# Two networks in one kernel: the gating's offset, the group norm and the masks of the rwkv stage, and who makes the third part of w_lo

## What is computed

```python
def _chunked_sgu(u, v, ln_g, ln_b, w_s, b_s):
    ...
    vn = ((vf - mu) * lax.rsqrt(var + SGU_LN_EPS)).reshape(bsz, t, A_WIDTH)
    vn = (vn * ln_g + ln_b).astype(v.dtype)
    ...
    mixed = jnp.einsum('gts,bcsgd->bctgd', wm, vc) + b_s.T[:, :, None]
    return u * mixed.reshape(bsz, t, A_WIDTH)
...
    y = _rwkv7_scan(rh, wh, kh, vh, kk, ah)
    ym = jnp.mean(y, axis=-1, keepdims=True)
    yv = jnp.mean(jnp.square(y - ym), axis=-1, keepdims=True)
    y = ((y - ym) * lax.rsqrt(yv + RWKV_GN_EPS)).reshape(bsz, t, B_WIDTH)
    y = y * gn_g.astype(jnp.float32) + gn_b.astype(jnp.float32)
    bonus = jnp.sum(rh * kh * r_k.astype(jnp.float32), axis=-1, keepdims=True) * vh
    y = (y + bonus.reshape(bsz, t, B_WIDTH)) * g.astype(jnp.float32)
```

## Time and profile before

| | |
|---|---|
| median of 3 runs | 2133.46 us (2132.8 to 2133.58) |
| the profiled execution | 2138.42 us, its span 2136.6 us |
| granted PE clock, mean | 0.984 of full speed |
| busy: PE, DVE, ACT, POOL | 2036.4, 1579.4, 1150.2, 447.4 us |
| delta's projection, rwkv stage, sparse's projection, from the span's start | about 206 to 296, 1088 to 1300, 1498 to 1594 us |

### The profile page before, as it was taken

One profiled execution on the slowest core, in us unless ns is written; L12 is line 12 of the kernel. 1 busy time (PEld: TensorE's weight loads), 2 busy tenths in 40 slices (PEclk: granted clock), 3 DMA queues, 4 the chain that ended last, 5 costly groups with the idle time before them and its releaser, 6 DMA issues.

```text
span 2136.6 us, 31970 instructions
## 1 busy us (share of the span) xinstructions
PE 2036.4 (95%) x11858; PEld 1778.4 (83%) x11858; DVE 1579.4 (74%) x2157; ACT 1150.2 (54%) x1687; POOL 447.4 (21%) x211
## 2 busy tenths in 40 slices
PE   7999989999999999999999989999987999999997
PEld 6888877888888899888888978888975888888885
DVE  5777886677777778677768476777675488888887
ACT  5445543544454455645455425445445577777775
POOL 2222213232322210133222432323320300000000
PEclk9999999999999999999999999999997999999998
DMA  8555420456555653355543005555450488888895
GB/s 336 186 196 168 152 105 14 169 192 193 190 177 182 198 169 141 138 189 195 187 158 119 1 1 181 193 190 193 158 178 15 166 332 326 326 325 324 326 327 194
DMA packets 73396, 401.23 MB, mean 188 GB/s; under 512 B 8256, under 2 KB 8384, under 8 KB 41152
## 3 DMA queue, kind: packets, MB, share of 16 engines
q1 hardware_dynamic: 72848, 398.07, 53.8%
q10 hardware_dynamic: 432, 1.57, 0.2%
HBM read 398.57 MB, written 1.05 MB: 187 GB/s over the span
## 4 chain that ended last, share of the span: by engine, by line
PE 77%; DVE 12%; PEld 4%; ACT 4%; issue 2%; POOL 1%; DMA 0%; SPq 0%; ACTq 0%; PEldq 0%; DVEq 0%; POOLq 0%
PE psum L737 17%; PE psum L306 13%; PE psum L307 13%; PE psum L308 12%; PE psum L741 9%; DVE w_lo L290 3%; PE psum L958 2%; ACT w_hi L283 2%; PE psum L946 2%; PE psum L320 2%; PE psum L2759 1%; PEld psum L306 1%; PEld psum L308 1%; PEld psum L307 1%; POOL w_lo L296 1%
## 5 line engine op out<-in xcount | busy, mean ns | idle before, releaser
L290 DVE TENSOR_TENSOR w_lo<-ring,w_hi 128x1024 fp32r<-128x1024 f32 x498 | 754.3, 1544 | 185.4 <-ACT w_hi L283 183.9
L283 ACT ACTIVATE w_hi<-ring 128x1024 fp32r<-128x1024 f32 x744 | 739.9, 1051 | 236.5 <-PEq L500 131.3
L296 POOL TENSOR_TENSOR w_lo<-ring,w_hi 128x1024 fp32r<-128x1024 f32 x153 | 381.4, 2493 | 1135.7 <-ACT w_hi L283 1135.7
L737 PE MATMUL psum<-fT,w_hi 128*128 128x512 f32 x1760 | 423.7, 392 | 12.9 <-DVE w_lo L290 10.4
L737 PEld LDWEIGHTS psum<-fT,w_hi 128*128 128x128 f32 x1760 | 330.4, 189 | 84.7 <-issue 7.5
L306 PE MATMUL psum<-w_hi,hT_hi 128*128 128x384 f32 (+4 forms) x896 | 321.7, 359 | 19.8 <-POOL w_lo L296 6.0
L308 PE MATMUL psum<-w_hi,hT_lo 128*128 128x384 f32 (+4 forms) x896 | 310.6, 347 | 0.0
L307 PE MATMUL psum<-w_lo,hT_hi 128*128 128x384 f32 (+4 forms) x896 | 310.3, 346 | 0.0
L306 PE MATMUL psum<-w_hi,act_hi 128*128 128x512 f32 x616 | 242.4, 394 | 5.4 <-DVE act_lo L835 4.6
L307 PE MATMUL psum<-w_lo,act_hi 128*128 128x512 f32 x616 | 241.2, 392 | 0.0
L308 PE MATMUL psum<-w_hi,act_lo 128*128 128x512 f32 x616 | 240.0, 390 | 0.0
(11 more groups left out here) (484 smaller groups left out, 2455.1 us busy)
## 6 DMA issues: line engine op xcount, KB each, us to landing
ring<-in_stream SPq DMA_DIRECT2D x249, 1024.0 KB, 5.6
ring<-in_stream SPq DMA_DIRECT2D x248, 512.0 KB, 4.3
tables<-in_tables SPq DMA_DIRECT2D x1, 2261.0 KB, 19.8
gain_row<-in_gains ACTq DMA_DIRECT2D x3, 512.0 KB, 4.8
rows<-in_rows SPq DMA_DIRECT2D x1, 1288.0 KB, 22.7
X<-in_x SPq DMA_DIRECT2D x1, 1024.0 KB, 5.0
result<-X SPq DMA_DIRECT2D x2, 512.0 KB, 3.4
columns<-in_columns SPq DMA_DIRECT2D x1, 993.0 KB, 14.9
```

The lines of the kernel that those rows point to most:

```text
L283: act.activation(part(w_hi, g, i), ring[:, k, i * PART:(i + 1) * PART], ACT.Copy) \
L290: dve.tensor_tensor(part(w_lo, g, i), ring[:, k, i * PART:(i + 1) * PART], part(w_hi, g, i).bitcast(F32), ALU.subtract) \
L296: pool.tensor_tensor(part(w_lo, g, 2), ring[:, k, 2 * PART:STEP], part(w_hi, g, 2).bitcast(F32), ALU.subtract) \
L737: pe.matmul(psum[:, 4 + 2 * (s % 2) + o, :], w[0][:, o, k, :], fT[:, k, :, :].rearrange("p a c -> p (a c)"), start=k == 0, stop=False, ski ...
```

## The change

Delta and sparse: the third part of w_lo is made by DVE in the projection's steps (`lasts`), and POOL waits until DVE is done. rwkv: the row sums of the gating's weights and the level made of them go; PE adds the product of the weights with ln_b in the same accumulation, POOL multiplies the gate's input by ln_g, and DVE adds sgu_b and multiplies by u in one operation per group out of PSUM. Result y is centred while it is copied from PSUM, with the mean reduced from PSUM. Half 0's variances and the norm of its first tile move into rwkv1's levels (`ahead`, before a level's U). A of half 1 is masked, and its first AM made, in rwkv0's last level. State, right side, solution and results of half 0 and matrices L, R, B move between rwkv1's levels; many `keep_warm` go; the turned tiles are issued one by one; the bonus on ACT moves to rwkv0's levels.

```diff
+        def inverse_begin(dve, A, AM):
             dve.tensor_tensor(AM[:, :, :], A[:, :, :], over(table("level")[:, 0:P], 8), ALU.mult).then_inc(*inverse.vector())
...
             for l in range(1, LEVELS):
+                if l in ahead:
+                    ahead[l]()
...
         def delta_pool(pool, at):
-            proj_pool(pool, first_step[at], len(D_KINDS))
+            pool.wait_ge(lo_last_ready, first_step[at] + len(D_KINDS))
...
-            proj_copies_vector(dve, "delta", at, D_KINDS, d_place, between)
+            proj_copies_vector(dve, "delta", at, D_KINDS, d_place, between, lasts=range(len(D_KINDS)))
...
         def sparse_pool(pool, at):
-            proj_pool(pool, first_step[at], len(N_KINDS) + SPARSE_C)
+            pool.wait_ge(lo_last_ready, first_step[at] + len(N_KINDS) + 1)
+            proj_pool(pool, first_step[at] + len(N_KINDS), SPARSE_C)
...
-                        {3: lambda: rotate(0), 4: lambda: rotate(1), 6: windows}, ahead=True)
+                        {3: lambda: rotate(0), 4: lambda: rotate(1), 6: windows}, ahead=True, lasts=range(len(N_KINDS)))
...
-            b = open_bank(pe, "rwkv sgu rows")
-            for g in range(4):
-                ins = pe.matmul(b[:, g:g + 1], col("sgu_w")[:, g * P:(g + 1) * P], ones[:, 0:1], start=True, stop=True)
-            ins.then_inc(*rwkv.tensor("rwkv sgu rows"))
...
+            def gating(t, gs):
+                b = open_bank(pe, f"rwkv sgu {t}") if gs[0] == 0 else bank(f"rwkv sgu {t}")
+                pe.wait_ge(*after(f"rwkv sgu scaled {t}"))
+                for g in gs:
+                    pe.matmul(b[:, g * P:(g + 1) * P], col("sgu_w")[:, g * P:(g + 1) * P], r_tok[:, t, 512 + g * P:512 + (g + 1) * P], start=True, stop=False)
+                    ins = pe.matmul(b[:, g * P:(g + 1) * P], col("sgu_w")[:, g * P:(g + 1) * P], row("ln_b")[:, g * P:(g + 1) * P], start=False, stop=True)
...
             inverse_tensor(pe, "rwkv0", r_T, r_U[0], r_Y, r_AM, 4, meanwhile=lambda: (matrix(0, "B"), key_rows()),
-                           at_level={5: lambda: right_side(0, 0), 6: lambda: matrix(1, "A")})
...
+                           at_level={5: lambda: (right_side(0, 0), matrix(1, "A"))})
+            solved(0, 0, 2)
+            inverse_tensor(pe, "rwkv1", r_T, r_U[1], r_Y, r_AM, 0, meanwhile=lambda: (state(0), result(0, 0)),
+                           at_level={1: lambda: right_side(0, 1), 2: lambda: (solved(0, 1), matrix(1, "L")), 3: lambda: result(0, 1),
+                                     4: lambda: matrix(1, "R"), 5: lambda: (right_side(1, 0), matrix(1, "B"))})
+            gating(0, range(4))
             solved(1, 0)
+            gating(1, range(2))
             state(1)
             result(1, 0)
-            gating()
             right_side(1, 1)
+            gating(1, range(2, 4))
             solved(1, 1)
+            turn(0, 0)
             result(1, 1)
...
+            turn(1, 0)
+            turn(0, 4)
+
+            out_tensor(pe, "rwkv", at, after_first=lambda: turn(1, 4), turns=1, warm=6)
...
             solved(1, 0)
...
+            split_hi(act, g, g, freed=f"rwkv1 dU {LEVELS - 1} 1")
             right_side(1, 1)
...
+            root(0, 1)
             solved(1, 1)
...
+            out_scalar(act, at, "rwkv", "used rwkv sgu 0", rwkv, meanwhile=lambda: root(1, 1), ahead=True)
...
+            inverse_pool(pool, "rwkv0", r_A, r_AM, at_level={4: lambda: shifted(0), 5: lambda: gate_scaled(0), 6: lambda: gate_scaled(1)})
+            inverse_pool(pool, "rwkv1", r_A, r_AM, at_level={1: lambda: gated(0), 2: lambda: shifted(1), 3: lambda: gated(1), 4: lambda: scaled(0),
+                                                             5: lambda: scaled(1)})
...
             def result(half, c):
                 dve.wait_ge(*after(f"rwkv y {half} {c}"))
-                does(f"used rwkv y {half} {c}", dve.tensor_copy, O[:, c, 512 + 256 * half:768 + 256 * half], bank(f"rwkv y {half} {c}")[:, 0:SEQ])
+                y, mean = bank(f"rwkv y {half} {c}")[:, 0:SEQ], r_stat[:, 5, 8 * c + 4 * half:8 * c + 4 * half + 4]
+                does(None, dve.tensor_reduce, mean, groups(y, 64), AX.X, ALU.add)
...
+            def next_half():
+                dve.wait_ge(*after(f"rwkv0 Y {LEVELS - 1} 1"))
+                masked(1, "A")
+                settle()
+                inverse_begin(dve, r_A, r_AM)
...
+            inverse_vector(dve, "rwkv0", r_A, r_T, r_U[0], r_AM,
+                           meanwhile=lambda: (bonus_sums(), masked(0, "L"), masked(0, "R"), group_mean(), masked(0, "B")),
+                           at_level={4: group_scale}, ahead={LEVELS - 1: next_half})
+            inverse_vector(dve, "rwkv1", r_A, r_T, r_U[1], r_AM, begun=True, meanwhile=lambda: (state(0), result(0, 0)),
+                           at_level={2: lambda: masked(1, "L"), 3: lambda: result(0, 1), 4: lambda: masked(1, "R"), 5: lambda: masked(1, "B")},
+                           ahead={3: lambda: variances(0, 0), 5: lambda: variances(1, 0), 6: lambda: normalise(0, 0)})
+            gating(0)
+            normalise(1, 0)
             state(1)
...
             result(1, 0)
-            gating()
...
+            gating(1)
             variances(0, 1)
...
             g = first_step[at] + len(R_KINDS)
             split_lo(dve, g, g, (0,))
+            normalise(0, 1)
+            split_lo(dve, g, g, (1,))
+            turn(0, 0)
+            turn(0, 4)
             result(1, 1)
             variances(1, 1)
...
+            turn(1, 0)
             normalise(1, 1)
...
+            turn(1, 4)
```

More of the change, by code:

```diff
@@ L2051, in rwkv_tensor, with bonus @@
                 pe.matmul(b, r_pm[:, GATE, t * P:(t + 1) * P], col("g2"), start=True, stop=True).then_inc(*rwkv.tensor(f"rwkv g {t}"))
-            b = open_bank(pe, "rwkv bonus")
-            keep_warm(pe, b, 6)
-            pe.wait_ge(*after("rwkv rk"))
-            for t in range(TT):
-                for c in range(4):
-                    ins = pe.matmul(b[:, 8 * t + 2 * c:8 * t + 2 * c + 2], r_rk[:, c, t * P:(t + 1) * P], table("pair_sel"), start=True, stop=True)
-            ins.then_inc(*rwkv.tensor("rwkv bonus"))
+            def bonus():
+                b = open_bank(pe, "rwkv bonus")
+                keep_warm(pe, b, 2)
+                pe.wait_ge(*after("rwkv rk"))
+                for t in range(TT):
+                    for c in range(4):
+                        ins = pe.matmul(b[:, 8 * t + 2 * c:8 * t + 2 * c + 2], r_rk[:, c, t * P:(t + 1) * P], table("pair_sel"), start=True, stop=True)
+                ins.then_inc(*rwkv.tensor("rwkv bonus"))
             def matrix(half, name):
@@ L2079, in key_rows, with turn @@
                     ins.then_inc(*rwkv.tensor(f"rwkv {name}"))
[L2081 to L2088 removed]
+            def gating(t, gs):
[4 more added lines that the diff above has]
+                    ins = pe.matmul(b[:, g * P:(g + 1) * P], col("sgu_w")[:, g * P:(g + 1) * P], row("ln_b")[:, g * P:(g + 1) * P], start=False, stop=True)
+                if gs[-1] == 3:
+                    ins.then_inc(*rwkv.tensor(f"rwkv sgu {t}"))
+            def turn(t, q):
+                b = open_bank(pe, f"rwkv turn {t} {q}")
+                pe.wait_ge(*after(f"rwkv gated {t}" if q else f"rwkv sgu done {t}"))
+                for k in range(4):
+                    ins = pe.transpose(b[:, k * P:(k + 1) * P], O[:, t, (q + k) * P:(q + k + 1) * P], ident)
+                ins.then_inc(*rwkv.tensor(f"rwkv turn {t} {q}"))
             def heads(half, c):
@@ L2101, in right_side @@
                 if c == 0:
-                    pe.wait_ge(*after(f"rwkv masked {half}"))
+                    pe.wait_ge(*after(f"used rwkv L {half} 1"))
                 else:
-                    keep_warm(pe, b, 3)
                     pe.wait_ge(*after(f"rwkv s1 {half} 1"))
@@ L2110, in right_side, with solved @@
                 ins.then_inc(*rwkv.tensor(f"rwkv rhs {half} {c}"))
-            def solved(half, c):
+            def solved(half, c, warm=0):
                 b = open_bank(pe, f"rwkv sa {half} {c}")
-                keep_warm(pe, b, 2)
+                keep_warm(pe, b, warm)
                 for par in range(2):
@@ L2120, in solved, with result @@
                 ins.then_inc(*rwkv.tensor(f"rwkv sa {half} {c}"))
-            def result(half, c):
+            def result(half, c, warm=0):
                 b = open_bank(pe, f"rwkv y {half} {c}")
-                keep_warm(pe, b, 2)
+                keep_warm(pe, b, warm)
+                pe.wait_ge(*after(f"used rwkv B {half} 1"))
                 pe.wait_ge(*after(f"used rwkv sa {half} {c}"))
@@ L2440, in rwkv_vector, with bonus_sums @@
             does("rwkv decayed", dve.tensor_tensor, rec, rec, r_c[:, :, :], ALU.mult)
-            dve.wait_ge(*after("rwkv bonus"))
-            row_sums()
-            dve.wait_ge(*after("rwkv bonus"))
-            does("used rwkv bonus", dve.tensor_copy, r_bonus.rearrange("p t h -> p (t h)"), bank("rwkv bonus")[:, 0:16])
+            def bonus_sums():
```

(15 more changed lines are left out.)

98 lines of the change are left out of this document (21 added, 77 removed).

## The result

The changed kernel takes 2122.1 us (median of 5 runs, 2120.33 to 2125.21) against 2133.46: a ratio of 0.9950, 95% interval 0.9936 to 0.9965. Measured again (E5) it took 2123.09 against 2134.21, ratio 0.9946 (0.9932 to 0.9959). So it is faster by 11.4 and 11.1 us; 15.2 were forecast. The profiled execution took 2124.79 us for a span of 2122.7, against a span of 2136.6 before.

The account below looks back on a forecast made before the run. PE, busy 95% of the span, was taken as the bound, with DVE's chain setting stops in delta and rwkv's tail. 2133.46 less 3.2 (delta), 2.0 (sparse) and 10.0 (rwkv) gave 2118.3 us; range 2113.0 to 2123.5.

Parts of the forecast that it names:

- Delta, -3.2: Delta's projection: nine thirds move to DVE, each gives back 2.0 us; PE stops of 0.3 and 0.8 remain; saves 3.2.
- Sparse, -2.0: Sparse's projection: nine thirds move to DVE, PE starts at 1573.2 instead of 1575.17, fillers still at 1.2 GHz; saves 2.0.
- windows: Sparse's projection: DVE's two subtractions drop from 3.49 to 1.3 us without POOL, shrinking a 1.20 us stop to 0.3.
- the clock stays up: Rival, sparse: after a shorter stop the fillers may run at 2.4 GHz, 2.9 us more saved, 2115.4 us; chance 0.23.
- the stop for `rstd_row`: Sparse's projection: PE still stops about 3 us before this row's copy and resumes at 1528.1 as before.
- rwkv up to the last result: rwkv stage until its last result: fewer PE matmuls against new stops, ending at 1267.4, 2.3 us before 1269.7.
- new stops: rwkv before the last result: PE waits 1.6 for a PSUM bank, 0.7 for U, 0.35 for T, 1.7 for ACT.
- rwkv, the tail, -10.0: rwkv after the last result: shorter DVE chain, second output step at 1283.6 instead of 1293.54; rwkv's whole gain, 10.0 us.
- a single fall of the clock: Rival case, rwkv: one clock fall costs 1.7 to 3.5 us, giving 2120 to 2122; chance 0.19 shared with another rival.
- The stop (c): rwkv, ACT: `root(0,1)` stands ahead of `solved(1,1)` and waits for DVE's variances, holding the last result 1.7 us.
- Fillers as a pure saving: rwkv before the last result: removing 24 fillers at 0.22 us each takes 5.2 us off PE.
- The tail gives back: Rival, rwkv: work placed beside PE's levels collides, costing 5 us in all, 2123; chance 0.19 shared with one clock fall.

Follow-up runs that it names:

- E5: The changed kernel itself, measured again beside the variants and the kernel before: 2123.09 us, ratio 0.9946.
- E2: The changed kernel with delta's and sparse's thirds of w_lo back on POOL, so rwkv's edits alone: 2128.4 us, ratio 0.9968.
- E9: The kernel before with only delta's nine thirds of w_lo given to DVE: 2130.09 us, ratio 0.9984.
- E10: The kernel before with only sparse's nine thirds of w_lo given to DVE: 2131.01 us, ratio 0.9984.
- E7: The changed kernel with the tail's stops reordered away, half 1's A masked earlier, further ACT reordering, and `rstd_row` copied ahead of `w_lo` in sparse: 2111.77 us, ratio 0.9890.
- E3: The changed kernel with 14 more idle matmuls on PE, 6 before the last result and 8 before the first output tile: 2118.47 us, ratio 0.9915.
- E11: The changed kernel with one exchange on ACT, `solved(1, 1)` ahead of `root(0, 1)`: 2117.11 us, ratio 0.9917.
- E6: The kernel before with only the idle matmuls of rwkv that the change removes taken out: 2132.15 us, ratio 1.0001.
- E1: The kernel before with only delta's and sparse's thirds of w_lo given to DVE, rwkv as before: 2125.58 us, ratio 0.9952.

## Why the prediction was right, and where it was off

The sign and the range were right; the likeliest value was 3.8 us too low, and its parts were off by more, in both directions. That the total came this close is partly luck: rwkv gave 6.3 us alone (E2) for a term of 10.0, and the thirds 6.8 to 9.1 for terms of 5.2.

- **Delta, -3.2.** Right. Both stops were forecast to 0.1 us, no other took their place, each group of nine gave back the 2.0 us of the sum, the profile shows 3.8, and E9 measured 3.4 (1.5 to 5.3).
- **Sparse, -2.0.** The stops came as forecast (first gone, 2.94 for 3, 2.57 for 2.6, windows 1.29 for 1.3). The term missed the clock twice, in opposite directions. I priced the fillers at half the clock, and in six of ten profiles they ran at the full one, as the rival "the clock stays up" had it (2.9 more). And I took the stop for `rstd_row` as free because PE resumes at the same time, where it is 1.1 us longer and the clock falls behind it (1.7 less). 2.0 + 2.9 - 1.7 = 3.2; E10's profile shows 3.1 and its runs 3.4 (1.5 to 5.3). E7 shows what the stop was worth: 4.7 us, by moving one copy.
- **rwkv up to the last result.** The working holds: the last result was to end 103.8 us into the stage (1267.4 - 1163.6). In the changed kernel's profile the product behind it starts at 106.3 (1266.20 - 1159.89), in E3 at 103.0 (1262.60 - 1159.64). The difference is the early low stretch, 1166 to 1174, which costs the changed kernel's profile 3.1 us (first transposition of the inversion 13.66 us into the stage, 10.55 in E3). It comes and goes between executions of the same code, so its share in the median isn't known. Two slips in the working were small: its terms (4.3 off, 4.35 of new stops, 1.9 of old ones gone) give 1.9 us, not the 2.3 booked, and the fillers behind the last result were 5.7 us of PE's time before, not 3.
- **rwkv, the tail, -10.0.** The step that failed is the sentence that a single fall of the clock costs 1.7 to 3.5 us and deserves little weight because PE is over 95% busy. That share was the one ahead of the tail. In the tail itself PE has stops of 1.72, 2.41 and 2.16, with 4.4 us of products between the first two and 12.8 before the third, and the clock was at 0.53 to 0.57 there in both profiles of the changed kernel (0.69 in E2's, with the same stops). Price: from last result to second output step 21.8 us against 18.1 in E3 (3.7), and 16.9 us from there to the feed-forward against 15.4 before (1.6; E3, which kept the stop of 2.17, has this one too). With the clock up the term was right: 135.7 us of stage in E3, 135.3 forecast. Free of low stretches on both sides it holds too: E10's stage of the old code is 144.3, less 10.0 is 134.3, and E3's without its 1.6 is 134.1.
- **The stop (c) at ACT's root** was sized right (1.72) and judged wrong. I booked 1.7 us for it; E11 took it away and got 6.0, of which its profile ties 2.6 to the edit's place and 1.6 to the clock behind the second output step.
- **Fillers as a pure saving.** I took 5.2 us off for 24 of them. E6 shows that alone they are worth far less here: 3.1 came at the last result, 1.6 at the stage's end, and in the time 2.1 by the medians, none by the ratio.
- **The tail gives back** (POOL against DVE inside the levels): no U, T or mask is stretched. The one collision is the 1.64 us row; E7 took it away by making POOL's operand earlier.
- **The profiled execution** shows 13.9 us of span where the medians show 11. That is which executions were profiled: the one of before is 5.0 us above its median, the one of after 2.7. In the experts' part, where PE is the bound, the clock was low from 1656 to 1660 and from 1686 to 1691 in the first only; in the second it was low from 876 to 881.

What stays open: whether the halves add up. E1 and E2 (9.1 and 6.3) exceed the whole (11), but with E9 and E10 in E1's place the gap is within the intervals. E2's stage has a mean clock of 0.96 and the whole's 0.93 and 0.94, one profile and two, which would fit but doesn't prove it. Whether the lost fillers or the stop (c) started the tail's low stretch can't be told apart either: mending either one shortens it (to none in E3, to 1265 to 1269 in E11). One profile each is thin evidence for a clock that differs between executions; what carries the reading is that the times of E3 and E11 lie below E5's with intervals that don't overlap.

## What to carry to other kernels

Before idle matmuls are taken out, or a stop is put into a stretch where PE sets the time, list the stops around it and price the clock for that whole stretch, not for one stop: here three stops of 1.7 to 2.4 us, 6.3 in all, cost 5.3 more through the clock. A stop that an exchange in another engine's queue can remove is the first to try: `root` behind `solved` gave 6.0 us (E11), the `rstd_row` copy ahead of `w_lo` some 4.7 (E7). A stop that only moves, as that one did under the change, is not free if it grows. A filler inside a stop (E3) cost nothing that could be seen. Compare several executions before a gap between forecast and profile is explained: the granted clock of one stretch differs from one execution to the next.
